# A hybrid decoder layer on eight cores: loads and cache copies that wait for named transfers or stages

## The reference, cut to what matters

```python
h = rms_norm(x, norm_mix_g)
z = h @ w_in                       # columns: q 1024 | k 256 | v 256 | GLU value 1024 | GLU gate 1024
q = rope(rms_norm(q, q_norm_g), pos);  k = rope(rms_norm(k, k_norm_g), pos)
a = banded attention, window 128, one learned sink logit per head   # sample tokens: cache_k, cache_v
u = u_val * sigmoid(u_gate);  c = causal depthwise conv, width 31   # sample tokens: state_conv
c = silu(layer_norm(c))
x = x + concat(a, c) @ w_out
x = x + square(relu(rms_norm(x, norm_mlp_g) @ w_up)) @ w_down       # hidden 8192
```

## Time and profile before

| what | value |
|---|---|
| time, median of 3 runs | 1493.12 us (1440.69, 1493.12, 1494.52) |
| the profiled execution: time | 1438.56 us |
| its span on the slowest core (core 3) | 1437.0 us |
| spans of the eight cores | 1424.4 to 1437.0 us |
| granted TensorE clock, core 3 | 0.965 of full speed |
| TensorE busy | 1319.4 us, 92% |
| VectorE busy | 742.7 us, 52% |
| ScalarE busy | 280.1 us, 19% |
| moved by DMA | 130.96 MB, mean 91 GB/s |

### The profile page before, as it was taken

The page is one execution under the profiler, slowest core; times in us unless marked ns, Lnnn a source line. Parts: engine busy times, 40 slices in busy tenths (PEclk is TensorE's granted clock), DMA queues, the critical chain, the costliest instruction groups (busy, mean ns, idle before and its releaser), DMA issues.

```text
span 1437.0 us, 22372 instructions; the slowest of 8 cores (1424.4 to 1437.0 us)
## 1 busy us (share of the span) xinstructions
PE 1319.4 (92%) x9016; PEld 826.9 (58%) x9016; DVE 742.7 (52%) x851; ACT 280.1 (19%) x429; POOL 112.4 (8%) x200
## 2 busy tenths in 40 slices
PE   3456979999879999999999999999999999999996
PEld 1122435555446666666666666666666666666664
DVE  3580785666546642544634535435446345354464
ACT  2350244565223541010010010000100100100000
POOL 1230000000001010000000010010000000100000
PEclk7787989999989999999999999999999999999998
DMA  9795006455953976255164263452541633624009
GB/s 219 199 164 93 1 1 112 85 108 98 202 130 56 148 110 112 35 99 89 30 118 74 45 107 54 75 99 38 99 88 30 118 69 49 105 50 82 16 9 227
DMA packets 57336, 130.96 MB, mean 91 GB/s; under 512 B 19064, under 2 KB 22012, under 8 KB 57212
## 3 DMA queue, kind: packets, MB, share of 16 engines
q0 software_dynamic: 38880, 90.74, 39.8%
q1 hardware_dynamic: 18356, 38.80, 10.2%
HBM read 202.73 MB, written 10.35 MB: 148 GB/s over the span
## 4 chain that ended last, share of the span: by engine, by line
PE 83%; DMA 9%; DVE 3%; issue 2%; SPq 1%; ACT 1%; POOL 0%; DVEq 0%; ACTq 0%; POOLq 0%
PE psum L621 83%; DMA arena<-xt 4%; DMA arena<-wq 3%; DVE arena L585 3%; DMA arena<-wo 2%; DMA arena<-arena 1%; SPq L920 1%; ACT arena L581 1%; PE psum L625 0%; SPq L568 0%; DVE arena L598 0%; POOL arena L568 0%; ACT L581 0%; DVEq L379 0%; ACT arena L603 0%
## 5 line engine op out<-in xcount | busy, mean ns | idle before, releaser
L621 PE MATMUL psum<-arena 128*128 128x344 bf16 (+5 forms) x8924 | 1314.9, 322 | 102.3 <-DMA arena<-wkv 25.9
L621 PEld LDWEIGHTS psum<-arena 128*128 128x128 bf16 (+2 forms) x8924 | 821.2, 99 | 590.0 <-issue 165.8
L585 DVE TENSOR_TENSOR arena<-psum,arena 128x1032 f32<-128x1032 f32 (+8 forms) x408 | 426.3, 1050 | 244.4 <-PE psum L621 204.1
L585 DVE TENSOR_TENSOR arena<-arena 128x1032 bf16<-128x1032 bf16 (+11 forms) x364 | 287.3, 807 | 401.2 <-ACT arena L581 382.9
L581 ACT ACTIVATE arena<-psum 128x512 bf16<-128x512 f32 (+7 forms) x150 | 116.0, 787 | 804.1 <-PE psum L621 803.1
L581 ACT ACTIVATE arena<-arena 128x352 f32<-128x352 f32 (+11 forms) x237 | 147.0, 647 | 159.9 <-DVE arena L585 91.2
L568 POOL DMA_DIRECT2D arena<-wup x64 | 33.8, 529 | 409.9 <-PE psum L621 409.9
L568 POOL DMA_DIRECT2D arena<-wdn x64 | 34.0, 534 | 375.5 <-PE psum L621 373.8
L598 DVE TENSOR_SCALAR arena<-arena 128x1160 bf16<-128x1160 f32 (+2 forms) x25 | 19.4, 777 | 32.6 <-DMA arena<-xt 31.6
L603 ACT COPY arena<-psum 128x1024 bf16<-128x1024 bf16 (+5 forms) x18 | 13.4, 771 | 74.7 <-PE psum L625 69.8
L568 POOL DMA_DIRECT2D arena<-wo x16 | 11.3, 704 | 146.3 <-PE psum L621 146.3
(11 more groups left out here) (10 smaller groups left out, 7.2 us busy)
## 6 DMA issues: line engine op xcount, KB each, us to landing
arena<-wdn POOLq DMA_DIRECT2D x64, 512.0 KB, 11.7
arena<-wup POOLq DMA_DIRECT2D x64, 512.0 KB, 6.7
arena<-xt SPq DMA_DIRECT2D x16, 580.0 KB, 9.4
arena<-arena SPq DMA_DIRECT2D x128, 65.8 KB, 4.6
arena<-xt SPq DMA_DIRECT2D x16, 516.0 KB, 16.0
yt<-arena SPq DMA_DIRECT2D x16, 514.0 KB, 9.1
arena<-wu POOLq DMA_DIRECT2D x16, 512.0 KB, 7.4
arena<-wo POOLq DMA_DIRECT2D x16, 512.0 KB, 9.2
```

Of the source, the lines that this page charges most:

```text
L585: return P.add(eng, lambda e: e.tensor_tensor(out=out.ap, in0=in0.ap, in1=in1.ap, op=op), reads=[in0, in1], writes=[out], cost=cost(eng, o ...
L621: return P.add("pe", lambda e: e.matmul(out.ap, lhsT.ap, rhs.ap, start=start, stop=stop), reads=[lhsT, rhs], writes=[out], cost=c)
```

## The change

Nothing is computed differently. Transfers are given more to wait for.

- `par` and `cst` wait for the third x block, `tab` for the sixth.
- The first four `wu` loads wait each for one of the last four `wq` loads.
- `sct` (the convolution state, into `FS`), `ckt` and `cv` wait for the last `wq` load.
- The three copies in memory (`nks`, `nvs`, `ncs`) are issued after the last matmul of `up_group(0)`.
- The second load of x (`xt_load`) waits for the last dense job of GLU group 3.

```diff
-    def wstream(src_ap, tag, m):
+    def wstream(src_ap, tag, m, after=()):
...
-            "wst%d" % i)
+            "wst%d" % i, after=after)
...
-            dma("sp", PAR(), R(par_d), "par")
-            dma("sp", CST(), R(cst_d), "cst")
+            dma("sp", PAR(), R(par_d), "par", after=[xd[2]])
+            dma("sp", CST(), R(cst_d), "cst", after=[xd[2]])
...
-            dma("sp", TABIN(), R(tab_d.rearrange("p (a b c) -> p a b c", a=2, b=10)), "tab")
+            dma("sp", TABIN(), R(tab_d.rearrange("p (a b c) -> p a b c", a=2, b=10)), "tab", after=[xd[5]])
...
+    wqd = []
     for kc in range(16):
-        dma("pool", WQ(kc), R(wq_d[kc]), "wq%d" % kc, after=[xd[15]] if kc >= 2 else [xd[13]])
+        wqd.append(dma("pool", WQ(kc), R(wq_d[kc]), "wq%d" % kc, after=[xd[15]] if kc >= 2 else [xd[13]]))
...
-    wu = [wstream(wu_d[order[i]], "wu", 128) for i in range(4)]
+    wu = [wstream(wu_d[order[i]], "wu", 128, after=[wqd[12 + i]]) for i in range(4)]
...
-    dma("sp", FS((0, 8), (0, SPC), (0, 30)), R(sct), "fs")
-    dma("sp", R(nks[:, 0:127, :]), R(ck[:, 1:128, :]), "d2d", group=True, final=True)
-    dma("sp", R(nvs[:, 0:127, :]), R(cv[:, 1:128, :]), "d2d", group=True, final=True)
-    dma("sp", R(ncs[:, :, :]), R(scv[:, 1:30, :]), "d2d", group=True, final=True)
-    dma("pool", KTS((0, SPC), (0, 2), (0, 127)), R(ckt), "cks", group=True)
-    dma("pool", CVB(p=(0, 127)), R(cv[:, 1:128, :].rearrange("s k d -> k s d")), "cks", group=True)
+    dma("sp", FS((0, 8), (0, SPC), (0, 30)), R(sct), "fs", after=[wqd[15]])
+    dma("pool", KTS((0, SPC), (0, 2), (0, 127)), R(ckt), "cks", group=True, after=[wqd[15]])
+    dma("pool", CVB(p=(0, 127)), R(cv[:, 1:128, :].rearrange("s k d -> k s d")), "cks", group=True, after=[wqd[15]])
...
         u_done(c)
+        if c == 3:
+            gate_xt = [P.streams["pe"][-1]]
...
-        dma("sp", XT(dc), R(xt_d[dc][:, MC0:MC0 + NM]), "xt%d" % dc)
+        dma("sp", XT(dc), R(xt_d[dc][:, MC0:MC0 + NM]), "xt%d" % dc, after=gate_xt)
...
     up_group(0)
+    late = [P.streams["pe"][-1]]
+    dma("sp", R(nks[:, 0:127, :]), R(ck[:, 1:128, :]), "d2d", group=True, final=True, after=late)
+    dma("sp", R(nvs[:, 0:127, :]), R(cv[:, 1:128, :]), "d2d", group=True, final=True, after=late)
+    dma("sp", R(ncs[:, :, :]), R(scv[:, 1:30, :]), "d2d", group=True, final=True, after=late)
```

## The result

| what | before | after |
|---|---|---|
| the profiled execution: time | 1438.56 us | 1400.96 us |
| its span (slowest core) | 1437.0 us (core 3) | 1399.4 us (core 2) |
| granted TensorE clock of that core | 0.965 | 0.980 |
| median of the runs | 1467.34 us (4 runs) | 1403.72 us (4 runs) |

The ratio of after to before is 0.9734, 95% interval [0.9698, 0.9769]: about 38 us less of 1437. The forecast was 45 us off the profiled execution's 1438.56, 3.1%; it came down by 37.6, 2.6%, and 1400.96 lies inside the stated range.

What follows compares the result with a forecast made beforehand. TensorE, busy 92%, sets the span, and transfer order bounds the start. Gains of 19 (x loop) and 27 (to the first q tiles) less 1 (copies) take 45 us off 1438.56: 1394 us, own range 1383 to 1408, 8 in 10 within 1382 to 1418.

Steps and rivals of the forecast that it cites:

- The x loop: Loading x blocks at the start: last block lands at 56 instead of 75.25 us, 19 us gained, bounds 13 to 25.6.
- The tables' waits: x loop: waits of `par`, `cst`, `tab` hold SyncE for nothing; the tables still cost 7.25 us, as now.
- From the last block to the first q tiles: Stretch after the x loop: three things go, together 27 us gained, bounds 18 and 29.
- The wait for `wq`: TensorE before the 72 q matmuls: the 22.6 us wait goes, with the last `wq` 8 us early.
- the long multiply: VectorE's last x-block multiply, 4.58 us beside the issue of `cv`, falls to 0.82; 3 of 3.76 us counted.
- The k chain: VectorE ends it 28.6 us after the last block against TensorE's 35, cover 6; rival that it delays TensorE: about 1407, chance 0.12.
- The moved issue of `cv`: At the k chain's end on VectorE: costs up to 3.8 us, or nothing by the skill's rule, inside the cover either way.
- The step that failed: Next q tiles: `sct`, `ckt`, `cv` land there, not needed before the GLU loop; no cost entered in the sum.
- My own sign of being wrong: Wrong if x blocks exceed 3.5 us each, a VectorE or key-copy wait replaces `wq`'s, or later stages lengthen.
- The copies in the MLP: First up groups: `wup` delayed, cost 0 to 5 us, taken 1; rival of full 16 us loss, 1410, chance 0.06.
- The second x loads: Four loads moved to the end of GLU group 3, some 10 us of transfer: cost 0 to 4 us, taken 0.
- The clock: Stages after the start: rival that fuller early work lowers the later granted clock, 1438 to 1460 us, chance 0.03.

Runs made afterwards that it cites:

- experiment 2: Kernel before with only the three copies in memory moved behind `up_group(0)`: 0.9934 of the kernel before, 1419 to 1439 us.
- 3: Changed kernel with the three copies in memory free again, going out behind the fourth x block: 0.9836 of the kernel before, 1411.1 to 1413.5 us.
- 10: Changed kernel with `cv` on its own semaphore and the four `wu` loads free again: 0.9717 of the kernel before, 1387.6 to 1395.0 us.
- 11: Changed kernel with `cv` on its own semaphore and `par`, `cst`, `tab` free again: 0.9646 of the kernel before.
- 4: Changed kernel with `sct`, `ckt` and `cv` free again, ahead of the last fourteen `wq` loads: 0.9831 of the kernel before, 1410.6 to 1413.4 us.
- 6: Changed kernel with `sct`, `ckt`, `cv` free again and `cv` cut into 112 and 15 partitions: 0.9642 of the kernel before, 1385.0 to 1388.6 us.
- 9: Kernel before with only its `cv` load cut into 112 and 15 partitions: 0.9873 of the kernel before, 1415.0 to 1419.9 us.
- 1: Changed kernel with the `cv` load counting on a semaphore of its own: 0.9650 of the kernel before, 1383.7 to 1388.0 us.
- 5: Changed kernel with the `cv` load cut into 112 and 15 partitions, semaphore still shared: 0.9623 of the kernel before, 1381.8 to 1387.8 us.
- 7: Changed kernel with `cv` on its own semaphore and the second x loads' wait for GLU group 3 undone: 0.9634 of the kernel before.
- 8: Changed kernel with `cv` on its own semaphore and the twelve later x loads behind the last GLU product: 1372.17 us, one execution, no ratio.
- 12: Changed kernel with `cv` cut in two, later x loads behind the last `U4` transfers, copies behind `up_group(1)`: 0.9571 of the kernel before, 1372.0 to 1375.1 us.

## Why the prediction was right and wrong

**The x loop** was right in mechanism and a little small: 22.0 us gained for 19. The copies are worth what the 19.0 us between `tab` and the fifth block said, which are 16 without one x block: 15.5 (experiment 2) and 16.1 us (3). The term of this sum that was mis-sized is `wu`: I took 0.8 us for two loads that cost 6 to 7 (10). The tables' waits are worth nothing (11), as costed.

**From the last block to the first q tiles** the sum of 27 came out as 26.8: from 75.25 to 143.45 before, from 53.20 to 94.62 after. The wait for `wq` and the long multiply went as said. Of the loads that I named in its way, `cv` alone counts (4, 6, 9); `sct`, `ckt`, the second x loads and `wu` together are left with at most the 4.0 us of experiment 9. The k chain stayed in its cover: `fin_k` waited 0.91 us for VectorE. The moved issue of `cv` did meet a VectorE instruction, the cast of 82.61, 3.89 us where the same cast took 0.28 at 107.36. The Trainium skill, page "SBUF — State Buffer", section "Who interferes with whom", names casts among the operations that can lock with GpSimd, and has tensor_tensor meet only GpSimd's reads. The rows agree, as the product at 82.09, beside the same issue, kept its 0.41 us. The prediction took that rule to mean no cost for the k chain, but the chain ends in a cast.

**The step that failed** is that the three cache loads could be moved back at no cost: "`sct`, `ckt` and `cv` land in the stretch of the next q tiles, where only `wu` is loaded", and, a paragraph earlier, "nobody needs these before the GLU loop". I asked who issues behind these loads and not who reads them, and took the reader's place in the program, GLU group 4, for its place on the queue. The reader is a VectorE copy which the planner puts as early as its inputs allow, and it stood among the q tiles in the trace of before, at 145.48, with nothing to wait for. Moving the loads behind `wq` moved the end of `cv` from 117 to 119 us while the q tiles moved 48.8 us forward, and the copy blocked the q chains. The term taken as 0 was 13.6 us: 11.1 of waiting, and the slower matmuls behind it with small waits, 2.5. Experiments 1 and 5 take it away in two ways and give 12 and 16 us. My own sign of being wrong came true with it: a wait for VectorE, among the next q tiles, behind the place where the wait for `wq` had stood.

**The copies in the MLP** cost 1.50 us in the changed kernel for 1 taken. Of the ten kernels that have them behind `up_group(0)`, four wait there for `wup`, 0.9 to 3.1 us, and six do not. **The second x loads** cost and gain nothing that can be measured (7), as taken. **The clock** did not fall: 0.980 after 0.965.

The account closes: 22.0 + 26.8 − 13.6 = 35.2 us at the start of the GLU loop's first matmuls, and the 1246.1 us from there to the end before became 1243.7, 2.4 more: 37.6. Without the failed step the change brings 50 to 54, as experiments 1 and 5 show. That 1400.96 us came out inside the range is in part luck: no term stood for the 13.6 us, and 3.0 of them were made up by the x loop and 2.4 behind it.

**A row read wrongly.** The nine tenths of the DMA engines' row are not at the start alone: the earlier trace rows has them in the 11th and the 14th slice too, 359 to 395 and 467 to 503 us. In the first of these begins the wait of 9.26 us for `U4`, which the change left as it was and which the order of experiments 8 and 12 takes away.

## What to carry to other kernels

When a load is moved later, list its readers by their place on the queue, not in the program text, and look at what each wait really counts: a cheap early reader on a busy engine, or a count shared with a slow neighbour, turns a hidden transfer into a stall of everything behind it. Before gating loads against each other, look for the one whose time to landing is out of proportion to its bytes: here cutting that load in two gave half the gain of the change, and made one of its gates needless. A gate inside a loop that is bound by bytes gives nothing; taking bytes out of it does.

## What the runs showed of the hardware

- A cast load of 254 KB to 127 partitions took 30.9 to 45.9 us to land in the ten kernels that have it whole, and some 4.6 us to issue; while only it ran, 12 GB/s were moved at a mean busy share of 0.09 of 16 engines. In parts of 112 and 15 partitions it took 9.9 to 16.9 us and 1.3 to 1.6 us to issue. The Trainium skill, page "DMA: Bandwidth & Descriptors", section "Why a DMA increments its semaphore by 16 and not by 1", has a copy of 127 partitions run on one engine and notes that this queue spreads some. The busy share, about one and a half engines, and the packets that went hardly more than one at a time (5) are near the first. No row here shows the engines apart, so that is argued, while the effect of the partition count is shown (5, 6, 9).
- Loads issued behind such a load on the same queue landed only behind it: of fourteen `wq` loads issued by 64.2 us the first landed at 89.6, 1.2 us after `cv`, and the last at 106.9, with 13 to 16 GB/s moved from 98 to 102 us (4).
- Three copies in memory, 1.48 MB, held the loads behind them for 16 us (2, 3), more than twice their bytes' time at 211 GB/s.
- SyncE's issue of a transfer of 4 KB took 16.57 us right behind `sct`, which has rows of 120 bytes, and 6.5 to 16.2 us in eight other kernels with that order; where `sct` had gone out over 30 us before, it took 0.3 us (five kernels). `cv` is not what held it: with `cv` cut it took 15.30 and 13.66 us (5, 12). SyncE's timeline in the changed kernel:

```profile
81.70 0.69 SPq L568 DMA_DIRECT2D arena<-sct  x1
82.60 16.57 SPq L568 DMA_DIRECT2D nks<-arena  x1
```
